# Token rows apart at the end of the projections, and five short reorderings, in a two-block transformer kernel

## What is computed

```
def first_block(x, ...):
    for layer in range(DEPTH):
        proj = rms_norm(x, norm_gain[layer]) @ w_in[layer]
        ...
        mixed = gates[:, :, 0, :] * y_a + gates[:, :, 1, :] * y_b
        x = x + mixed @ w_out[layer]
    return rms_norm(x, final_gain)

def second_block(x, p, ...):
    for i in range(DEPTH):
        u = rms_norm_2(h, norm_attn[i]) @ w_in[i]
        ...
        mix = jnp.concatenate([o_a, o_b, o_c, o_d], axis=-1)
        h = h + mix @ w_out[i]
        c = rms_norm_2(h, norm_ffn[i])
        if i % 2 == 0:
            h = h + swiglu(c, ffn_w_gate[i // 2], ffn_w_up[i // 2], ffn_w_down[i // 2])
        else:
            h = h + moe_swiglu(c, moe_router[i // 2], moe_w_gate[i // 2], moe_w_up[i // 2], moe_w_down[i // 2])
        gate = jax.nn.sigmoid(rms_norm_2(h, ple_norm[i]) @ ple_w_gate[i])
        h = h + (p[i] @ ple_w_proj[i]) * gate
    return h
```

## Time and profile before

| | |
|---|---|
| median of 3 runs | 2643.92 us |
| lowest, highest | 2643.88, 2646.43 us |
| profiled execution | 2646.02 us |
| its span | 2644.5 us |
| mean granted TensorE clock | 0.972 of full |
| expert stage (first gate product to the next norm) | 1641 to 2600 us |

### The profile page before, as it was taken

One profiled execution on the slowest core, in us unless ns is written; L12 is line 12 of the kernel. 1 busy time (PEld: TensorE's weight loads), 2 busy tenths in 40 slices (PEclk: granted clock), 3 DMA queues, 4 the chain that ended last, 5 costly groups with the idle time before them and its releaser, 6 DMA issues. The chain is left out here.

```text
span 2644.5 us, 47407 instructions
## 1 busy us (share of the span) xinstructions
PE 2550.8 (96%) x21427; PEld 1429.2 (54%) x21427; DVE 642.5 (24%) x1352; ACT 488.0 (18%) x830; POOL 134.3 (5%) x331
## 2 busy tenths in 40 slices
PE   9999999999999988999999988999999999999999
PEld 8666557766554774444445764353444535353444
DVE  3534523433533532000024432000101001010002
ACT  1521321421322432001013430100000000000001
POOL 4011000011000210000001200000000000000000
PEclk9999999998999988999999888999999999999999
DMA  7421333421335412444446114999999999999992
GB/s 244 132 76 55 127 117 119 152 74 56 112 120 130 135 49 90 153 145 141 151 133 174 63 43 160 375 363 380 355 385 346 377 364 369 373 369 371 361 375 89
DMA packets 192349, 542.29 MB, mean 205 GB/s; under 512 B 29168, under 2 KB 57232, under 8 KB 192144
## 3 DMA queue, kind: packets, MB, share of 16 engines
q1 hardware_dynamic: 178848, 536.95, 56.3%
q10 hardware_dynamic: 12992, 1.22, 0.4%
q0 software_dynamic: 304, 1.05, 0.1%
HBM read 538.12 MB, written 1.05 MB: 204 GB/s over the span
## 5 line engine op out<-in xcount | busy, mean ns | idle before, releaser
L399 PE MATMUL psum<-ring,hT 128*128 128x512 f32 (+3 forms) x1632 | 685.8, 578 | 13.1 <-ACT area L746 7.0
L399 PEld LDWEIGHTS psum<-ring,hT 128*128 128x128 f32 x1632 | 309.0, 197 | 348.1 <-issue 322.9
L2604 PE MATMUL psum<-ring,area 128*32 128x448 f32 x4608 | 439.5, 539 | 1.7 <-DVE area L2780 1.1
L2604 PEld LDWEIGHTS psum<-ring,area 128*32 128x32 f32 x4608 | 149.9, 110 | 283.8 <-issue 279.9
L632 PE MATMUL psum<-hT,ring 128*128 128x256 f32 x768 | 169.5, 384 | 0.0
L632 PEld LDWEIGHTS psum<-hT,ring 128*128 128x128 f32 x768 | 148.1, 193 | 21.4 <-issue 1.0
L2623 PE MATMUL psum<-area 128*32 128x256 f32 x2688 | 149.8, 380 | 2.0 <-ACT area L2753 2.0
L2623 PE MATMUL psum<-ring,area 128*32 128x256 f32 x2688 | 151.5, 380 | 0.0
L2604 PE MATMUL psum<-area 128*32 128x448 f32 x1536 | 147.3, 539 | 0.0
L2623 PEld LDWEIGHTS psum<-area 128*32 128x32 f32 x2688 | 85.7, 110 | 60.2 <-ACT area L2753 3.9
L2623 PEld LDWEIGHTS psum<-ring,area 128*32 128x32 f32 x2688 | 84.9, 110 | 57.1 <-issue 2.9
(11 more groups left out here) (526 smaller groups left out, 2354.0 us busy)
## 6 DMA issues: line engine op xcount, KB each, us to landing
ring<-in_w_in_dram SPq DMA_DIRECT2D x92, 1024.0 KB, 5.1
ring<-in_moe_w_gate_dram SPq DMA_DIRECT2D x96, 896.0 KB, 6.6
ring<-in_moe_w_up_dram SPq DMA_DIRECT2D x96, 896.0 KB, 8.2
area<-in_moe_w_down_dram SPq DMA_DIRECT2D x112, 512.0 KB, 7.4
ring<-in_moe_w_down_dram SPq DMA_DIRECT2D x112, 512.0 KB, 6.9
area<-in_moe_w_gate_dram SPq DMA_DIRECT2D x32, 896.0 KB, 7.4
area<-in_moe_w_up_dram SPq DMA_DIRECT2D x32, 896.0 KB, 8.3
ring<-in_w_out_dram SPq DMA_DIRECT2D x16, 1024.0 KB, 5.1
```

What stands on the lines that cost most here:

```text
L399: last = nc.tensor.matmul(acc(g)[:, t, 0:d["n"]], lhs(kk, t), w[:, k, :], start=kk == 0, stop=kk == d["nk"] - 1)
L2604: last = nc.tensor.matmul(PS[32 * j:32 * j + 32, 3 * p + b, 0:PIECE], XG[:, k, 32 * b:32 * b + 32], expert_slot(j0 + j // 2, GROUP * (j % ...
```

## The change

Six edits.

1. The last half product of the right columns runs all four contraction blocks for token half 0, then all four for token half 1 (`mix_pe`), and signals `rows_done` in between, where the transposes of the left half stand. VectorE adds token half 0 on that signal and token half 1 at the end (`right_half_dve`, `gained_residual_dve`). The last down product of the feed-forward is split in the same way.
2. In norm 0, VectorE squares the quarter (0, 1) as well, and ScalarE one fewer.
3. In `MIXER_PLAN` one `f` stands ahead of the last attention transposes instead of behind them.
4. In `post_act` a `root_table` stands behind the first square.
5. In `ple_dve` of layer 0, multiply and add of the right columns run per token half, the first on a signal of the first product. The counts of `ple_unit` move by one.
6. In `pass_dve` the selection is made for expert 0 ahead of the signal to TensorE, and for the other seven behind the shares.

```
@@ squared_by_vector
-            return () if n == 0 else ((0, 1), (1, 1)) if n == 8 else ((1, 1),)
+            return ((0, 1), (1, 1)) if n in (0, 8) else ((1, 1),)
@@ gained_residual_dve
-            for half, g in enumerate(group(name, L)):
...
+            left, right = group(name, L)
+            c = slice(0, 512)
+            s.eng.wait_ge(sem("weights_used"), used(TILES[left]["end"] - 1))
+            s.after(nc.vector.tensor_tensor(X[:, :, c], X[:, :, c], acc(left), ALU.add).then_inc(sem("x_updated"), 1), "x_updated")
+            s.eng.wait_ge(sem("final_gain"), 16)
+            s.after(nc.vector.tensor_tensor(XGAIN[:, :, c], X[:, :, c], bc(RFINAL[:, c].unsqueeze(1), [P, T, 512]), ALU.mult)
+                    .then_inc(sem("xf_ready"), 1), "xf_ready")
+            c = slice(512, 1024)
+            s.eng.wait_ge(sem("rows_done"), ROWS[name][L])
+            s.do(nc.vector.tensor_tensor(X[:, 0, c], X[:, 0, c], acc(right)[:, 0, :], ALU.add))
+            s.do(nc.vector.tensor_tensor(XGAIN[:, 0, c], X[:, 0, c], RFINAL[:, c], ALU.mult))
+            s.eng.wait_ge(sem("weights_used"), used(TILES[right]["end"] - 1))
+            s.after(nc.vector.tensor_tensor(X[:, 1, c], X[:, 1, c], acc(right)[:, 1, :], ALU.add).then_inc(sem("x_updated"), 1), "x_updated")
+            s.after(nc.vector.tensor_tensor(XGAIN[:, 1, c], X[:, 1, c], RFINAL[:, c], ALU.mult).then_inc(sem("xf_ready"), 1), "xf_ready")
@@ rstd_dve
             for half, t in squared_by_vector(n):
+                if n == 0:
+                    x_half(s.eng, n, half)
@@ mix_pe, half_product
-                for kk in range(4):
-                    for t in range(T):
...
-                    if n is not None and (g, h, kk) == (right, 1, 1):
-                        norm_pe(pe, n, 0)
+                rows_apart = (g, h) == (right, 1)
+                for kk, t in sorted(itertools.product(range(4), range(T)), key=lambda i: i[::-1] if rows_apart else i):
...
+                    if rows_apart and (kk, t) == (3, 0):
+                        last.then_inc(sem("rows_done"), 1)
+                        if n is not None:
+                            norm_pe(pe, n, 0)
@@ new, called by residual_dve and ffn_dve for the right columns
+        ROWS = dict(out=(1, 2), out2=(3, 6), ffn=(4, None))
+        def right_half_dve(s, rows, last, products):
+            xs = X[:, :, 512:1024]
+            s.eng.wait_ge(sem("rows_done"), rows)
+            s.do(nc.vector.tensor_tensor(xs[:, 0, :], xs[:, 0, :], products[:, 0, :], ALU.add))
+            s.eng.wait_ge(sem("weights_used"), used(last))
+            s.after(nc.vector.tensor_tensor(xs[:, 1, :], xs[:, 1, :], products[:, 1, :], ALU.add).then_inc(sem("x_updated"), 1), "x_updated")
@@ MIXER_PLAN (its end)
-        ...agafaavgffaffapgpvgpp"
+        ...agafaavgfffafapgpvgpp"
@@ post_act
                     .then_inc(signal("m_osq_early"), 1), "m_osq_early")
+            root_table(s)
             yield
@@ ffn_pe
-            last.then_inc(sem("ffn_left"), 1)
+            last.then_inc(sem("rows_done"), 1)
             down(12, 1).then_inc(sem("weights_used"), 1)
             norm_pe(pe, n + 1, 0)
-            down(13, 1).then_inc(sem("weights_used"), 1)
+            down(13, 1, [0]).then_inc(sem("rows_done"), 1)
+            down(13, 1, [1]).then_inc(sem("weights_used"), 1)
@@ ple_pe and ple_dve, layer 0
-                ple_unit(pe, L, 1, 0, 6)
+                ple_unit(pe, L, 1, 0, 6).then_inc(sem("ple_unit"), 1)
...
+                s.eng.wait_ge(sem("ple_unit"), 2)
+                s.do(nc.vector.tensor_tensor(TMP[:, 0, :], SGP[:, 0, 512:1024], PS[:, 6, :], ALU.mult))
+                s.do(nc.vector.tensor_tensor(X[:, 0, 512:1024], X[:, 0, 512:1024], TMP[:, 0, :], ALU.add))
                 s.eng.wait_ge(sem("weights_used"), used(TILES[group("pp", L)[1]]["first"]))
-                add(X[:, :, 512:1024], TMP, SGP[:, :, 512:1024], PS[:, 6:8, :], "x_updated")
+                add(X[:, 1, 512:1024], TMP[:, 1, :], SGP[:, 1, 512:1024], PS[:, 7, :], "x_updated")
@@ pass_dve
-            for t in range(T):
-                ins = nc.vector.tensor_tensor(PALL[:, t, 0:NE, :], bc(IOTA.unsqueeze(1), [P, NE, CAP]),
-                                              bc(SLOT[:, t].unsqueeze(2), [P, NE, CAP]), ALU.is_equal)
...
+            def chosen(t, e0, e1):
+                return nc.vector.tensor_tensor(PALL[:, t, e0:e1, :], bc(IOTA.unsqueeze(1), [P, e1 - e0, CAP]),
+                                               bc(SLOT[:, t, e0:e1].unsqueeze(2), [P, e1 - e0, CAP]), ALU.is_equal)
+            s.do(chosen(0, 0, NE if r else 1))
+            s.after(chosen(1, 0, NE if r else 1).then_inc(ms("placed"), 1), "moe_placed")
             if r:
                 clear_dve()
             else:
                 shares_dve(s)
+                for t in range(T):
+                    s.do(chosen(t, 1, NE))
```

More of the change, by code:

```diff
@@ L7 @@
+import itertools
 import math
@@ L1400, in half_product @@
                 w = half_view(load, (4, 512))
-                for kk in range(4):
-                    for t in range(T):
-                        last = nc.tensor.matmul(acc(g)[:, t, :], mixed(k)[:, 4 * h + kk, t * P:(t + 1) * P], w[:, kk, :],
-                                                start=h + kk == 0, stop=h == 1 and kk == 3)
-                    if n is not None and (g, h, kk) == (right, 1, 1):
-                        norm_pe(pe, n, 0)
+                rows_apart = (g, h) == (right, 1)
+                for kk, t in sorted(itertools.product(range(4), range(T)), key=lambda i: i[::-1] if rows_apart else i):
+                    last = nc.tensor.matmul(acc(g)[:, t, :], mixed(k)[:, 4 * h + kk, t * P:(t + 1) * P], w[:, kk, :],
+                                            start=h + kk == 0, stop=h == 1 and kk == 3)
+                    if rows_apart and (kk, t) == (3, 0):
+                        last.then_inc(sem("rows_done"), 1)
+                        if n is not None:
+                            norm_pe(pe, n, 0)
                 last.then_inc(sem("weights_used"), 1)
@@ L1429, in mix_act @@
                     .then_inc(sem("mixT_ready"), 1), "mixT_ready")
-        def residual_dve(s, name, L):
[L1432 to L1437, removed]
+        ROWS = dict(out=(1, 2), out2=(3, 6), ffn=(4, None))
[5 more added lines that the diff above has]
+            s.after(nc.vector.tensor_tensor(xs[:, 1, :], xs[:, 1, :], products[:, 1, :], ALU.add).then_inc(sem("x_updated"), 1), "x_updated")
+        def residual_dve(s, name, L):
+            left, right = [TILES[g] for g in group(name, L)]
+            s.eng.wait_ge(sem("weights_used"), used(left["end"] - 1))
+            xs = X[:, :, 0:512]
+            s.after(nc.vector.tensor_tensor(xs, xs, acc(group(name, L)[0]), ALU.add).then_inc(sem("x_updated"), 1), "x_updated")
+            right_half_dve(s, ROWS[name][L], right["end"] - 1, acc(group(name, L)[1]))
         def gate_dve(s, half):
@@ L2252, in ffn_pe, with down @@
             ple_turn_pe(pe, L, 6)
-            def down(i, dh):
+            def down(i, dh, rows=range(T)):
                 w = half_view(DOWN[L] + i, (2, D))
                 for k in range(2):
-                    for t in range(T):
+                    for t in rows:
                         last = nc.tensor.matmul(PS[:, 2 * dh + t, :], HFT[:, 2 * i + k, t * P:(t + 1) * P],
@@ L2304, in ffn_dve @@
                 s.after(nc.vector.tensor_tensor(HTOK[f % 2], SGF[f % 2], acc(g), ALU.mult).then_inc(sem("gemm_out_dve"), 1), "gemm_out_dve")
[L2305 to L2311, removed]
+            s.eng.wait_ge(sem("rows_done"), ROWS["ffn"][L])
+            s.after(nc.vector.tensor_tensor(X[:, :, 0:512], X[:, :, 0:512], PS[:, 0:2, :], ALU.add).then_inc(sem("x_updated"), 1), "x_updated")
+            right_half_dve(s, ROWS["ffn"][L] + 1, DOWN[L] + 13, PS[:, 2:4, :])
             s.eng.wait_ge(sem("ple_unit"), 1)
@@ L2406, in ple_dve @@
                 for c in range(2):
-                    s.eng.wait_ge(sem("ple_unit"), 5 + c)
+                    s.eng.wait_ge(sem("ple_unit"), 6 + c)
                     cols = slice(512 + 256 * c, 768 + 256 * c)
@@ L2556, in pass_dve @@
                 s.do(nc.vector.tensor_scalar(SLOT, SLOT, -float(CAP), None, ALU.add))
-            for t in range(T):
-                ins = nc.vector.tensor_tensor(PALL[:, t, 0:NE, :], bc(IOTA.unsqueeze(1), [P, NE, CAP]),
-                                              bc(SLOT[:, t].unsqueeze(2), [P, NE, CAP]), ALU.is_equal)
-                if t == 0:
-                    s.do(ins)
-                else:
-                    s.after(ins.then_inc(ms("placed"), 1), "moe_placed")
+            def chosen(t, e0, e1):
[3 more added lines that the diff above has]
+            s.after(chosen(1, 0, NE if r else 1).then_inc(ms("placed"), 1), "moe_placed")
             if r:
```

17 lines of the change are left out of this document (4 added, 13 removed).

## The result

| | before | after |
|---|---|---|
| median | 2645.07 us (5 runs, 2643.88 to 2647.22) | 2621.68 us (5 runs, 2618.16 to 2632.64) |
| ratio | | 0.9914 [0.9900, 0.9927] |
| profiled execution | 2646.02 us (span 2644.5) | 2618.16 us (span 2616.6) |
| mean granted clock of it | 0.972 | 0.980 |

The change saves 23.4 us; the forecast was 10.9 from the median, with a range down to 2627.5. A second set of five runs of the changed kernel gave a ratio of 0.9900 [0.9886, 0.9915]. The lines of the profile that answer to the rows of before follow.

The account below looks back on a forecast made before the run. TensorE, busy 96% of the span, was taken to bound the kernel, so only its pauses and lowered clock could give. Terms summed to 10.9 us, from the median 2643.9 to 2633.0; forecast 2633, range 2627.5 to 2639.5.

Parts of the forecast that it names:

- the add of 0.69: Four output projections: only a second 512-element add of 0.69 remains instead of 1.22, saving 0.53 us each, 2.1 in all.
- the copy that hides the feed-forward's: Feed-forward: VectorE waits for a next-stage product and copies it, TensorE waits for that copy, so the split add saves 0.
- the pause of 1.04: Ahead of the last attention transposes: moved fill step cuts TensorE's 2.76 us pause to about 1.0, saving 1.73 per layer.
- the load without a drain: Mixer head norm, both layers: moving ScalarE's root table load saves 1.28 us each, 2.6 in all, with no drain of 1.38.
- the pair of selections at 0.55: Expert routing: expert 0's two selections take 0.55 us ahead of the gather instead of 1.95 for all eight, saving 1.4.
- the expert stage did not become the weights': Rival, chance 0.03: expert weight transfers become last if they sink under 367 GB/s; at 350 GB/s 46 us more, 2679.
- The step sum: Whole kernel: 2.1 + 0 + 0.25 + 1.05 + 3.5 + 2.6 + 1.4 = 10.9 us saved, without clock.
- The first norm: Squares moved to VectorE let its sum start some 1.5 us sooner, but TensorE's own work leaves only 0.25 us saved.
- The clock: Layer 0's last attention: 1.7 us more for the profiled execution from no clock loss, perhaps nothing for the median one.
- the clock gives more: Rival, chance 0.10: shorter TensorE pauses spare some stretches at 1.2 GHz, giving 2633 - 6 = 2627 us.
- no pause goes away whole: Argument against the rival of a larger clock gain: the change removes no whole pause, only part of one in the mixer.
- three or four fewer: Size of the clock rival: three or four fewer low-clock stretches, each costing up to 1.7 us, give 6 us.

Follow-up runs that it names:

- same_before: The kernel before, run again unchanged; median 2643.23 us over 11 runs, ratio 1.0000.
- longer_norms: The kernel before with a useless 360-element sum on VectorE ahead of the last right-half add at four output projections; 2657.81 us, ratio 1.0050.
- rows edit: Token halves apart in the four output projections and the feed-forward; alone on the kernel before, 2638.88 us, ratio 0.9976.
- The groups: The edits split in three, each run alone on the kernel before and each left out of the kernel after; alone ratios 0.9976, 0.9986, 0.9993.
- the rest group: First norm's squares, per-layer gate by token halves and selection of expert 0; alone on the kernel before, 2644.42 us, ratio 0.9993.
- The mixer's two lines: The moved plan letter `f` and the moved `root_table`; alone on the kernel before, 2639.71 us, ratio 0.9986.

## Why the prediction was wrong

*What bounds the kernel, and the steps.* Right. Ten of eleven terms came out within 0.1 us; the add of 0.69, the copy that hides the feed-forward's, the pause of 1.04, the load without a drain, the pair of selections at 0.55 were all seen where they were expected, and the expert stage did not become the weights': 1003.5 us from its first product to the end in both profiles. The step sum was checked by a second route: brought to equal time at the low level (150 us) with a slope of 0.35 to 0.47, the ten runs of the changed kernel have a mean of 2634 to 2638 us, and 81 of before 2646. That is 8 to 12 us, around the 10.9.

*The table load.* 1.28 us each, as booked. The Trainium skill's page ScalarE: Activation LUTs (What ACT_TABLE_LOAD costs) gives 2.66 with a drain. The trace after disagrees as before did: the square ends at 1550.77, the load runs from 1550.79 to 1552.07 and the next function starts at 1552.08, and what was saved is 1.28.

*The first norm.* Booked 0.25, gave nothing that shows. The diff moves two of the four squares to VectorE, not one as the second of the six edits is worded. VectorE's sum came at 7.09 instead of 7.91, 0.8 sooner and not 1.5. From TensorE's first transpose to the scale products it takes 3.96 and 4.25 us in the two profiles of before (before, `same_before`), 4.25 and 4.00 in those of after. The weight load did wait 0.28 for the reciprocal in the profile of before, but not in `same_before`, where TensorE's own work ends last.

*The clock.* This is the term that was mis-sized: 0 (or 1.7 for the profiled execution) booked, some 12 to 16 us measured (22.7 and 26.4 less 10.6). The rival "the clock gives more" named the mechanism, but had 0.10 and stopped at 6 us. Two sentences of it failed. "Against: no pause goes away whole" took for granted that a pause a third shorter behaves like the pause before; `longer_norms` shows that 0.56 us on a pause of 1.39 changes the clock, in the other direction, and the gate that cutting a pause from 1.79 to 0.70 removes the stretch behind it. And "three or four fewer" at up to 1.7 us each was read from the one short stretch of the earlier trace rows; the two that gave most are 10 and 14 us long and gave 3.8 us (at 410) and 5.4 us (at 640). The profile of before had them all: a mean clock of 0.972 stood in the prediction as 148 us at 1.2 GHz, at 0.37 us for each of them some 55 us of possible gain, next to a sum of 10.9. The Trainium skill's page TensorE: Matmul & The Clock Gate (HAM oscillation) says that pauses between bursts take the clock away and gives an example with pauses of 3 to 5 us for loads. The trace agrees on the direction; no pause of TensorE in before is that long (the longest is the 2.76 of the earlier trace rows), and half a microsecond more or less on 1.4 moved the clock.

*The spread.* The prediction took the spread from three runs of before (2.6 us). The 81 runs of before beside the experiments span 2640.1 to 2653.3, with a standard deviation of 3.2 us; the changed kernel's ten span 2617.2 to 2632.6, with 5.5. In the profiles, places such as 242, 410 and 640 fall or hold from one execution to the next. A range for such a kernel needs that width.

*What stays open.* Why, at equal pauses, one execution keeps the clock at 242, 410 and 640 and the next does not; why the stretch at 640, where no pause changed, becomes rarer with the rows edit; and so how much each edit contributes at each place. That shorter pauses give clock is shown at the gate and, with the sign turned, by `longer_norms`; for the rest of the surplus the pauses are the likely cause, and the distance between the pauses is a rival that no run tests. The groups overlap: their single gains (11.9) and their joint gain (23 to 26) can't be divided among them. No run tried the plan letter and the table load apart.

## What to carry to other kernels

Read the granted clock of the windows before costing a change that shortens TensorE's pauses: each microsecond at the low level cost about 0.4 us here, and half a microsecond at four pauses, 2.1 us in sum, moved the time by three times that sum when cut from before, and by six times when added to it. Book the direct steps from the rows, and give the clock a term and a range of its own instead of a side case. Judge such edits together, not singly, and time them in many runs: the rest group alone gave 1.9 us, not clear of noise, and was worth 10 to 14 beside the others.

## What was not expected of the hardware

- The same instructions with the same pauses took 4.22 or 7.10 us in two executions of one kernel; the standard deviation of a run grew from 3.2 us (before, 81 runs) to 5.5 (after, 10 runs) while the median fell.
- Useless matmuls that cut norm 1's pauses from 0.85, 0.76 and 1.21 to 0.42, 0.32 and 0.34 us brought no gain in sum (0.9923 against 0.9900 and 0.9914), though the low stretch at 800 went.
- Time at the low level cost less than half its length (0.37 between two executions of the same kernel).
- The mixer's two lines alone left more time at the low level than before (154 us against 148, by the mean clocks) and took a stretch there behind norm 4 (1042 us) that before lacks; together with the rows edit it was gone.
